# Attention of a two-layer trunk: scores issued in odd steps, the products with the values in two blocks, and both token streams as one sequence of steps

## The reference

```python
m = jnp.maximum(scores.max(-1, keepdims=True), sink)   # branch A; B and C have no sink
e = jnp.exp(scores - m)
p = e / (e.sum(-1, keepdims=True) + jnp.exp(sink - m))
o = p @ v
y = (g_a * (o_a @ w_a) + g_b * (o_b @ w_b) + g_c * (o_c @ w_c)) @ w_out     # g: sigmoid gates
x = layer_norm(ALPHA * x + g1 * y)
```

## Time and profile before

| | before |
|---|---|
| median of 3 runs | 1769.73 us (1769.31 to 1771.0) |
| the profiled execution | 1767.51 us, its span 1765.7 us |
| PE busy | 1504.7 us, 85% of the span |
| PEld / DVE / ACT busy | 814.8 / 506.8 / 399.5 us |
| mean granted PE clock | 0.916 |

### The profile page before, as it was taken

How to read it: one execution, slowest core, us unless ns; L and a number is a source line. 1 busy time by engine, 2 the same in 40 slices (tenths; PEclk the granted TensorE clock), 3 DMA queues, 4 the chain that set the end, 5 groups by cost and what they waited for, 6 DMA issues and landing times.

```text
span 1765.7 us, 23068 instructions
## 1 busy us (share of the span) xinstructions
PE 1504.7 (85%) x9748; PEld 814.8 (46%) x9748; DVE 506.8 (29%) x1002; ACT 399.5 (23%) x856; POOL 23.3 (1%) x47
## 2 busy tenths in 40 slices
PE   7999998999988998899888798989976676676764
PEld 3543446888874343433222274568752333332322
DVE  0225576433552000011010454765630000000003
ACT  1213677222231010200000132864320001000000
POOL 1000000000000000000000100000000000000000
PEclk9999999999988999999999899999977768776767
DMA  9645921333557999999999921046989999999995
GB/s 365 243 180 242 384 83 63 111 90 101 191 218 286 421 421 421 421 421 420 422 421 422 327 84 48 1 142 196 358 326 421 421 421 421 420 421 420 421 421 225
DMA packets 101509, 522.69 MB, mean 296 GB/s; under 512 B 11024, under 2 KB 13344, under 8 KB 47136
## 3 DMA queue, kind: packets, MB, share of 16 engines
q1 hardware_dynamic: 97712, 509.97, 72.5%
q0 software_dynamic: 3392, 10.85, 1.8%
q10 hardware_dynamic: 304, 0.40, 0.1%
HBM read 520.04 MB, written 1.15 MB: 295 GB/s over the span
## 4 chain that ended last, share of the span: by engine, by line
PE 55%; SPq 23%; DMA 12%; DVE 6%; ACT 2%; issue 1%; DVEq 0%; ACTq 0%
PE psum L527 51%; SPq L1093 23%; DMA ring<-in_w_down 7%; PE psum L607 4%; DMA ring<-in_w_up 3%; DMA A<-in_w_down 2%; DMA ring<-in_w_ada 1%; ACT hT L1239 1%; DVE small L1706 1%; DVE PR L1725 1%; DVE X L1736 1%; DVE X L1737 1%; DVE X L1843 1%; DVE small L1711 0%; DVE stats L1849 0%
## 5 line engine op out<-in xcount | busy, mean ns | idle before, releaser
L527 PE MATMUL psum<-ring,A 128*32 128x256 f32 (+1 forms) x1920 | 278.6, 548 | 72.8 <-DMA ring<-in_w_up 40.6
L527 PE MATMUL psum<-ring_r,h_hi 128*128 128x512 f32 x704 | 218.2, 391 | 6.9 <-DVE h_lo L1743 5.8
L527 PE MATMUL psum<-A 128*32 128x256 f32 (+5 forms) x1152 | 185.4, 540 | 38.5 <-DMA A<-in_w_up 19.3
L527 PEld LDWEIGHTS psum<-ring,A 128*32 128x32 f32 (+1 forms) x1920 | 88.6, 137 | 249.0 <-issue 104.4
L1877 DVE TENSOR_TENSOR W<-W,psum 128x512 f32<-128x512 f32 (+1 forms) x32 | 17.7, 555 | 548.5 <-PE psum L527 548.5
L527 PE MATMUL psum<-ring,PR 128*32 128x256 f32 (+1 forms) x1080 | 143.4, 498 | 29.2 <-DMA ring<-in_w_down 29.1
L527 PE MATMUL psum<-ring,hT 128*128 128x512 f32 (+3 forms) x512 | 165.1, 476 | 3.0 <-DVEq L1497 1.2
L527 PE MATMUL psum<-ring_r,h_lo 128*128 128x512 f32 x384 | 149.7, 390 | 0.0
L527 PEld LDWEIGHTS psum<-ring_r,h_hi 128*128 128x128 f32 x704 | 132.1, 189 | 35.2 <-issue 6.6
L527 PEld LDWEIGHTS psum<-A 128*32 128x32 f32 (+3 forms) x1152 | 61.5, 143 | 126.2 <-issue 58.4
L527 PEld LDWEIGHTS psum<-ring,hT 128*128 128x128 f32 x512 | 85.7, 194 | 68.8 <-issue 66.6
(11 more groups left out here) (201 smaller groups left out, 1415.6 us busy)
## 6 DMA issues: line engine op xcount, KB each, us to landing
ring<-in_w_down SPq DMA_DIRECT2D x93, 1024.0 KB, 25.9
ring<-in_w_up SPq DMA_DIRECT2D x85, 1024.0 KB, 25.3
ring<-in_w_gate SPq DMA_DIRECT2D x80, 1024.0 KB, 25.3
ring<-in_w_ada SPq DMA_DIRECT2D x40, 1024.0 KB, 9.0
A<-in_w_up SPq DMA_DIRECT2D x40, 1024.0 KB, 26.0
A<-in_w_gate SPq DMA_DIRECT2D x38, 1024.0 KB, 26.4
ring<-in_w_in SPq DMA_DIRECT2D x36, 1024.0 KB, 5.1
A<-in_w_down SPq DMA_DIRECT2D x28, 1024.0 KB, 26.0
```

Of the source, the lines that this page charges most:

```text
L527: return nc.tensor.matmul(o, a, b, start=start, stop=stop, skip_group_check=True)
```

## The change

The two streams of layer 0 become one sequence of 64 units (`all_units`), so that `attention(l, step)` is called once for a layer and runs over 72 steps in layer 0 and 40 in layer 1. On PE every step begins with the transposes of unit i-3; odd steps then issue the scores of units i+1 and i+2 (units 0 and 1 ahead of the loop); even steps issue one half of the products with the values of a pair, the first half five steps after the pair's last unit and the second half seven; the modulation's products come last in a step. ACT copies O eight steps after the pair's last unit, between the exponential and the copy of T. The scores have banks 0 to 3, the transposes banks 4 and 5, and O shares bank 6 with the turns of the modulation, which in the attention are moved to steps 3 of 4. DVE's part differs only in the numbering of the units. Layer 1 has the same order over its 32 latent units.

```diff
@@ -29,6 +29,7 @@
 LN_EPS, RMS_EPS = 1e-5, 1e-6
 RING, SLOT = 9, 2048
 ADA_BANK, TURN_BANK = 7, 6
+SCORE_BANKS, TURNED_BANKS = (0, 1, 2, 3), (4, 5)
 GATE_COL = 1696
 
...
@@ -361,10 +362,20 @@
 
         def units(l, s):
 
-            return [(4 * j + 2 * q + h, j, h, q) for j in range(8) for q in (0, 1) for h in (0, 1)]
-
-        def unit_base(l, s):
-            return 32 * (2 * l + s) if l == 0 else 64
+            return [(s, 4 * j + 2 * q + h, j, h, q) for j in range(8) for q in (0, 1) for h in (0, 1)]
+
+        def all_units(l):
+            return [unit for s in streams(l) for unit in units(l, s)]
+
+        def unit_before(l, i, back):
+
+            s, u = all_units(l)[i - back][0:2]
+            return "T", l, s, u
+
+        def pair_before(l, i, back):
+
+            s, _, j = all_units(l)[i - 4 * back][0:3]
+            return "O", l, s, j
 
 
...
@@ -378,9 +389,10 @@
             ada_due.setdefault(at, {})["products"] = which + (n % 8,)
             if n % 8 == 7:
                 ada_due.setdefault(at, {})["move"] = which
-                ada_due.setdefault(at + 2, {})["turn"] = which
+                turn_at = at + 2 if n < QKV_TURNS else QKV_TURNS + (at + 2 - QKV_TURNS | 3)
+                ada_due.setdefault(turn_at, {})["turn"] = which
                 if which[1] == 2:
-                    ada_due.setdefault(at + 4, {})["rows"] = which[0]
+                    ada_due.setdefault(turn_at + 4 if n >= QKV_TURNS else turn_at + 2, {})["rows"] = which[0]
 
         def row_tiles(l):
...
@@ -680,57 +692,74 @@
...
+            def scores(l, pair):
+
+                for s, u, j, h, q in pair:
+                    br, first = PAIRS[j]
+                    t, nk = 2 * s + q, 4 if s else 2
+                    b = begin(("S", l, s, u), bank=SCORE_BANKS[u % 4])
+                    if br == "B":
+                        mm_in = qT["B"][0:QK_B, first + h, t * P:(t + 1) * P], kT["B"][0:QK_B, first + h, 0:nk * P]
+                    else:
+                        rows = slice(HD * h, HD * h + HD)
+                        mm_in = qT[br][rows, first, t * P:(t + 1) * P], kT[br][rows, 0:nk * P]
+                    if u % 4 == 0 and (j == 0 or PAIRS[j - 1][0] != br):
+
+                        for tt in range(4):
+                            drained(pe, (f"T{br}k" if br == "B" else f"T{br}r", l, tt))
+                            if br == "B" and not (l == DEPTH - 1 and tt < 2):
+                                drained(pe, ("TBq", l, tt))
+                    masked = br == "A" and s == 1
+                    ins = mm(psum[:, b, 0:nk * P], *mm_in, True, not masked)
+                    if not masked:
+                        end(ins, b)
+                for s, u, j, h, q in pair:
+                    if PAIRS[j][0] == "A" and s == 1:
+                        pe.wait_ge(masks_ready, 1)
+                        b = groups["S", l, s, u][0]
+                        at = 256 + P * (1 - q)
+                        end(mm(psum[:, b, at:at + P], ident16[:, :], mask16[:, q, :], False, True), b)
+
+            def values(l, unit, half):
+
+                s, u, j, _, _ = unit
+                nk = 4 if s else 2
+                if half == 0:
+                    for v in range(u - 3, u + 1):
+                        drained(pe, ("T", l, s, v))
+                    begin(("O", l, s, j), bank=TURN_BANK)
+                br, h0 = PAIRS[j]
+                for k in range(nk // 2 * half, nk // 2 * half + nk // 2):
+                    for h in (0, 1):
+                        col = HD * (h0 + h if br == "B" else h)
+                        p = pT[:, (2 * j + h) % 4, :].rearrange("p (k q) -> p k q", q=256)
+                        ins = mm(psum[HD * h:HD * h + HD, TURN_BANK, 0:256], V[br][:, k, col:col + HD], p[:, k, :],
+                                 k == 0, k == nk - 1)
+                if half:
+                    end(ins, TURN_BANK)
+
+            def attention(l, step):
+                us = all_units(l)
+
+                turn[0] += (TURNED_BANKS[0] - turn[0]) % 6
+                scores(l, us[0:2])
+                for i in range(len(us) + 8):
+                    if i == LAST_TURN_AT:
                         qkv(l, LAST_TURN)
+                    if 3 <= i < len(us) + 3:
+                        s, u = us[i - 3][0:2]
+                        pe.wait_ge(prob_ready, 64 * l + i - 3 + 1)
+                        transposes(("T", l, s, u), [prob[:, u % 4, k * P:(k + 1) * P] for k in range(4 if s else 2)],
+                                   bank=TURNED_BANKS[u % 2])
+                    if i % 2:
+                        scores(l, us[i + 1:i + 3])
+                    for half in (0, 1):
+                        back = 5 + 2 * half
+                        if i >= back and i - back < len(us) and us[i - back][1] % 4 == 3:
+                            values(l, us[i - back], half)
                     if l == 0:
                         ada_hook(step)
                     step += 1
                 return step
...
@@ -1071,8 +1100,7 @@
             step = QKV_TURNS
             for l in range(DEPTH):
                 qkv(l, PE_FIRST + QKV_NEXT if l else QKV_STEPS)
-                for s in streams(l):
-                    step = attention(l, s, step)
+                step = attention(l, step)
                 gates(l)
                 project_and_route(l)
...
@@ -1325,49 +1353,49 @@
                             b = filled(act, (kind + "r", l, t))
                             nc.scalar.copy(kT[kind[1]][:, cols], psum[:, b, 0:P]).then_inc(bank_drained[b], 1)
 
-            def attention(l, s, step):
-                nk = 2 if s == 0 else 4
-                us = units(l, s)
-                for i in range(len(us) + 5):
-                    if s == streams(l)[0] and i == LAST_TURN_AT:
+            def attention(l, step):
+                us = all_units(l)
+                for i in range(len(us) + 8):
+                    if i == LAST_TURN_AT:
                         qkv(l, LAST_TURN)
                     if i < len(us):
-                        u, j, h, q = us[i]
+                        s, u, j, h, q = us[i]
                         br, head = PAIRS[j][0], head_at(j, h)
+                        n = 512 if s else 256
                         b = filled(act, ("S", l, s, u))
-                        act.wait_ge(max_ready, unit_base(l, s) + u + 1)
-                        if u >= 4:
-
-                            filled(act, ("T", l, s, u - 4))
+                        act.wait_ge(max_ready, 64 * l + i + 1)
+                        if i >= 4:
+
+                            filled(act, unit_before(l, i, 4))
                         c4 = 64 + 4 * (u % 4)
                         if br == "A":
                             nc.scalar.activation(small[:, c4 + 1:c4 + 2], sink[:, head:head + 1], ACT.Exp,
                                                  bias=small[:, c4:c4 + 1])
-                        nc.scalar.activation(prob[:, u % 4, 0:nk * P], psum[:, b, 0:nk * P], ACT.Exp,
+                        nc.scalar.activation(prob[:, u % 4, 0:n], psum[:, b, 0:n], ACT.Exp,
                                              bias=small[:, c4:c4 + 1],
                                              accum_out=small[:, c4 + 2:c4 + 3]).then_inc(bank_drained[b], 1)
+                    if i >= 8 and us[i - 8][1] % 4 == 3:
+                        s, _, j, _, _ = us[i - 8]
+                        b = filled(act, ("O", l, s, j))
+                        nc.scalar.copy(oT[:, j, 256 * s:256 * s + 256], psum[:, b, 0:256]) \
+                            .then_inc(bank_drained[b], 1)
                     if l == 0:
                         ada_hook(step)
                     step += 1
                     if 3 <= i < len(us) + 3:
-                        u, j, h, q = us[i - 3]
+                        s, u, j, h, q = us[i - 3]
+                        nk = 4 if s else 2
                         b = filled(act, ("T", l, s, u))
-                        hd = 2 * j + h
-                        if hd >= 4:
-
-                            filled(act, ("O", l, s, (hd - 4) // 2))
-                        p = pT[:, hd % 4, :].rearrange("p (k q) -> p k q", q=256)
+                        if i - 3 >= 8:
+
+                            filled(act, pair_before(l, i - 3, 2))
+                        p = pT[:, (2 * j + h) % 4, :].rearrange("p (k q) -> p k q", q=256)
                         nc.scalar.copy(p[:, 0:nk, q * P:(q + 1) * P],
                                        psum[:, b, 0:nk * P].rearrange("p (k q) -> p k q", k=nk)) \
                             .then_inc(bank_drained[b], 1)
-                    if i >= 5 and us[i - 5][0] % 4 == 3:
-                        j = us[i - 5][1]
-                        b = filled(act, ("O", l, s, j))
-                        nc.scalar.copy(oT[:, j, 256 * s:256 * s + 256], psum[:, b, 0:256]) \
-                            .then_inc(bank_drained[b], 1)
-                    if s == 1 and i in EARLY_SPLITS_AT:
-
```

(7 more changed lines are left out.)

47 lines of the change are left out of this document (3 added, 44 removed).

## The result

The changed kernel takes 1771.70 us (median of 20 runs, 1768.4 to 1775.2), the kernel before beside it 1767.14 us (20 runs). The ratio is 1.0025, with a 95% interval of 1.0017 to 1.0033: slower by 4.4 us, where 1.8 us faster was forecast.

A forecast was written before the change was run, and what follows sets the result against it. PE's queue in the attention, with holes, was taken to bound the kernel. 6.5 - 12.9 + 3.0 + 0.6 + 1.0 (layer 1's start) = -1.8 us, so 1769.7 became 1767.9 us, range 1762.5 to 1773.0.

The forecast's parts named there:

- What bounds it: Layer 0 and 1 attention: a queue of PE with holes; an attention ending x earlier moves all that follows by x.
- The added groups, +6.5: Values in two blocks add PE work that nothing covers: 6.5 us, 4.1 in layer 0 and 2.4 in layer 1.
- The removed waits, -12.9: Banks by kind and the later O copy remove PE's waits: 12.9 us, 6.5 in layer 0, 6.4 in layer 1.
- what is late next, +3.0 and +0.6: New lateness in the attention: ACT's roundings of weights 3.0 us, turns of the modulation sharing bank 6 with O 0.6.
- (a): ACT's two roundings in each latent stream's last eight units: PE waits, bounds 0 and 5.6 us, taken 3.0.
- (b): Half blocks wait until DVE or ACT empties bank 6, shared with the modulation: bounds 0 and 2.0 us, taken 0.6.
- waits come back: Rival, 14%: half of the 12.9 is real lateness of exponentials, returning as waits for copies: +1.7, 1771.4 us.
- The bank of the values: Rival, 13%: first half blocks wait for ACT's copy of the previous pair's O from one bank: +6.0, 1773.9 us.
- The clock: Rival, 10%: layer 1 starts at the low clock for 4 us longer: +2.0 on the forecast, 1769.9 us.
- past 1107 us: Sign that the forecast is wrong: a low clock at layer 1's start lasting beyond this time.
- The scores' part: Scores a step ahead pass only modulation products and the projections' last turn; nothing gained in PE's queue, taken as 0.
- One sequence: Layer 0's streams joined: no PE wait at the seam beyond those counted, its work the same: 0.

The follow-up runs named there:

- the repaired kernel: The changed kernel with the old order at the start of an attention and ACT's roundings of weights in latent branch B: 1766.11 us, ratio 0.9996.
- the start as before: The changed kernel with scores of units 2 and 3 and modulation's step 3 back in the first wait, last turn in bank 5: 1769.48 us, 1.0017.
- the roundings in B: The changed kernel with ACT's two roundings of weights at units 14 and 18 (latent branch B) in place of 24 and 28: 1768.29 us, 1.0010.
- start + B: The changed kernel with the start of an attention as before and ACT's roundings in latent branch B: 1766.11 us, ratio 0.9996.
- start + B, one block and the copy at eight: start + B with the values' products in one block, ACT's copy of O left at step eight: 1773.99 us, ratio 1.0040.
- its two variants: The kernel before with the values' products in two blocks, 1771.37 us, 1.0028; the kernel before with roundings in latent branch B, 1767.09 us, 0.9998.
- the same one block: start + B with the values' products in one block: 1773.99 us with ACT's copy of O at step eight, 1763.58 us at step six.

## Why the prediction was wrong, by its own steps

**What bounds it.** Held. The attention is a queue of PE with holes, and the attention's length went through to the whole: 3.5 us of 4.3 in the profiled executions.

**The added groups, +6.5.** Right in mechanism and nearly in size: 3.97 us of PE work in layer 0 against 4.1. What was wrong is the sentence that nothing covers it. In the kernel before 1.5 of the 4.0 us went into PE's idle time; the ratio says 5.0 for both layers, with an interval that just holds 6.5, and in the repaired kernel the split cost 2.5.

**The removed waits, -12.9, and what is late next, +3.0 and +0.6.** This is the step that failed. The sum gave layer 0 a net of -6.5 + 1.5 + 0.6 = -4.4 us of idle time; measured is -0.1. The waits named after exponentials did go. The copies of T and O cost 2.1 + 1.3 + 0.3 = 3.7 us in their place and a mark of DVE ahead of a half block 0.3, together 4.0 where 2.1 was allowed; the wait of the first transpose, which was to stay, grew by 1.7 (see the clock, below). In the run with the start as before, which has a clock of 1.00 in all of layer 0, the waits in place of the old ones were 5.0 us:

```profile
PE psum L619 <- ACT W L1396: 2.9, 5, 1.3
...
PE psum L539 <- ACT B L1383: 1.3, 3, 0.6
```

with 0.3 and 0.3 as above and 0.2 for probabilities. In layer 1 they were 1.6 + 1.1 = 2.7. I had taken (a) at 3.0 for both layers, "since ACT gets a lead of about a step", while the view of stretches showed ACT busy 25.2 of 31.3 us. Moving the roundings measured the term: 2.5 us in layer 0 and 0.8 in layer 1. Together that is 3.3, close to the 3.0, but layer 0's share was 1.0 more than the 1.5 in the sum. What stayed in layer 0 with the roundings in B, 0.9 + 0.3 + 0.3 = 1.5 us, stands against the 0.6 of (b). The rival "waits come back" has the mechanism. It had 14%; "half of the 12.9 are real lateness" was low for layer 0. That its 1771.4 us is so near the measured time is luck: it stood for +1.7 us, and the change is +4.4.

**The bank of the values.** In the changed kernel a small term: 1.3 + 0.3 and 1.1 us, near the low end of its rival. In a neighbouring kernel it came true: with start + B, one block and the copy at eight the waits for the copy of O are 5.6 us in layer 1 alone. That its time is the rival's (1773.99 us against 1773.9) is chance, as that kernel differs in other parts too. What decided there wasn't whether ACT is late by 1.6 us now and then, but how many steps lie between the block and its copy.

**The clock.** Foreseen for layer 1 alone. There the wait of 4.13 us came as described, in answer to the earlier trace rows, and the low clock with it:

```profile
1104.11 1.09 PE L619 MATMUL psum<-cst,PR 128*128 128x128 f32 x4 [4.13 <-ACT A L1351]
1105.12 2.08 PE L539 MATMUL psum<-A 64*128 64x512 f32 x4
```

But the low clock didn't last longer, in answer to the earlier trace rows, before and after:

```profile
1096.30:1106.50 10.20, 9.01 (x31) 4.19 (x29) 7.99 (x26) 7.58 (x21) 0.00 (x0) 0.50 0.01 3
```

```profile
1099.50:1109.80 10.30, 6.17 (x23) 3.52 (x23) 7.61 (x23) 7.34 (x20) 0.00 (x0) 0.50 0.01 2
```

The attention of layer 1 as a whole starts 3.2 us later (mark at 1099.10 against 1095.90), and counted from the mark both low stretches run from 0.4 to 10.7 us. So "past 1107 us" was no sign of this rival. Filling the waits of layer 1 brings the clock to 1.00 throughout and is worth 0.9 us, where the rival had priced 2.0. In layer 0 I did not look, since the kernel before had 1.00 everywhere. But the scores and the modulation's work of the first steps passed the first wait there as well ("Only the modulation products and the last turn of the projections are passed. Nothing is gained in PE's queue; taken as 0"), and that made two short idle times one of 2.59 us, at 1.3 us. The scores' part at 0 was the second step that failed.

The Trainium skill ("TensorE: Matmul & The Clock Gate", section "HAM oscillation — how this bites in real kernels") says that a matmul stream whose waits are long enough starts each piece on the slow clock. This case agrees for the wait of 2.59 us, six times in six. But with waits of at most 0.88 us the clock fell as well, in two of the seven executions with the old start: the length of the last wait alone doesn't decide.

**One sequence.** 0 forecast, 0 measured.

**The numbers.** 1771.7 us lies within the range of 1762.5 to 1773.0, but that is luck. The forecast was counted from the median of 3 runs, 1769.7 us, and 20 runs of the same kernel gave 1767.14. The change itself, +4.4 us, lies outside the bounds of the sum, -6.4 to +3.2. "Slower" had a chance of 16% only. Two things would have raised it with what the trace showed: ACT's load in the last stretch set against the sum of the waits named ACT, and the order of work in the first four steps of layer 0 written out.

## What to carry to other kernels

A wait that ends with a loaded engine's instruction may be that engine's lateness, whatever resource it is named after. Then giving the resource its own banks moves the wait to the next thing the engine must do, as here for T and O, and taking work away from the engine, or moving it, is what helps. It may also be the place of the instruction in that engine's program, as with the copy at step eight; an edit to each tells the two apart. Where a change passes work over a wait, write out what is left to fill that wait: two short idle times made one can cost the clock as well. And when one part of a change is undone, its companions must be set for it: the same one block cost 1.0040 with the copy at step eight and gave 0.9982 with the copy at six.

## What was not expected of the hardware

The clock's fall isn't fixed by the wait. Behind each attention PE waits 2.89 us for the first rounded activations, the same in every one of the 14 profiled executions (one for each kernel of the table). In the 8 us that follow, the granted clock was 1.00 in six of them and 0.62 to 0.82 in eight for layer 0, 1.00 in four and 0.79 or 0.82 in ten for layer 1. The kernel before, as profiled, had 1.00 in both; the changed one had neither, here in layer 0:

```profile
289.11:297.11 8.00, 8.00 (x28) 6.45 (x29) 8.00 (x7) 8.00 (x8) 0.00 (x0) 0.79 0.30 121
```

A clock of 0.79 over 8 us is 1.7 us of PE work, about as much as each part of this change. It goes with the stretch behind the last gates, which is 2.0 us longer in the changed kernel: from the start of layer 1's last gates to the end the four executions with 1.00 took 603.3 to 604.1 us, and the ten with the low clock 604.2 to 607.1. Whether the fall there is chance stays open. The kernel before and its two variants had it in 1 of 6 cases, the changed kernel and its variants in 17 of 22, so the change may well bring it on; no run here tests that. The Trainium skill (the same page, section "The HAM clock gate (the "warmup" mystery)") says that the count of slow matmuls at a kernel's start differs from run to run of one kernel. No kernel was profiled twice here, so no run shows that; what the 28 cases here show is the middle of 14 different kernels. A term below about 2 us isn't to be read from one execution's span without a look at this clock.
